# Gating weights read eight hidden blocks at a time in runs of 1 KB, two scale rows parked in memory, activations packed to 352 columns

## The reference, cut to what matters

```python
def peer(xn, w_pq, sub_keys, u, v):
    q = (xf @ w_pq).reshape(t, PEER_HEADS, 2, PEER_HALF)
    sc = jnp.einsum("thpd,hpnd->thpn", q, sub_keys).astype(jnp.float32)
    vals, idx = lax.top_k(sc, PEER_TOPK)
    ...
    best, pos = lax.top_k(cand, PEER_TOPK)
    eidx = jnp.take_along_axis(cidx, pos, axis=-1)
    g = jax.nn.softmax(best, axis=-1).astype(xn.dtype)
    ...
        ue = jnp.take(u, it, axis=0)
        act = jax.nn.gelu(jnp.einsum("td,tkd->tk", xt, ue), approximate=False) * gt
        ve = jnp.take(v, it, axis=0)
        return jnp.einsum("tk,tkd->td", act, ve)
...
        h = h + gate2 * peer(n2, w_pq[l], sub_keys[l], peer_u[l], peer_v[l])
    return rms_norm(h, g_final)
```

## Time and profile before

| | us |
|---|---|
| median of 3 runs | 1630.06 |
| lowest, highest | 1626.07, 1630.55 |
| profiled execution | 1628.63 |
| its span | 1626.8 |
| TensorE busy in it | 1587.6 |
| VectorE busy in it | 1382.7 |
| ScalarE, GpSimd busy in it | 643.2, 565.3 |
| mean granted TensorE clock | 0.987 |

### The profile page before, as it was taken

One profiled execution on the slowest core, in us unless ns is written; L12 is line 12 of the kernel. 1 busy time (PEld: TensorE's weight loads), 2 busy tenths in 40 slices (PEclk: granted clock), 3 DMA queues, 4 the chain that ended last, 5 costly groups with the idle time before them and its releaser, 6 DMA issues.

```text
span 1626.8 us, 23629 instructions
## 1 busy us (share of the span) xinstructions
PE 1587.6 (98%) x7941; PEld 1313.7 (81%) x7941; DVE 1382.7 (85%) x2751; ACT 643.2 (40%) x950; POOL 565.3 (35%) x479
## 2 busy tenths in 40 slices
PE   6999999999999999999999999999999999999997
PEld 4887764675556899988889888898988898888886
DVE  6788867765999999978989898989988888988886
ACT  3334654241112666663333333333333333333333
POOL 0000000011555300015555455554545566656510
PEclk7999999989999999999999999999999999999999
DMA  9522215532212255589999999999999999999981
GB/s 370 188 106 78 78 53 204 221 144 70 90 67 85 99 207 190 206 286 367 375 370 359 368 365 369 364 369 363 358 344 353 344 350 361 344 348 346 362 292 61
DMA packets 144460, 417.89 MB, mean 257 GB/s; under 512 B 11520, under 2 KB 56576, under 8 KB 138624
## 3 DMA queue, kind: packets, MB, share of 16 engines
q1 hardware_dynamic: 96128, 247.01, 42.2%
q0 software_dynamic: 47104, 167.83, 27.2%
q10 hardware_dynamic: 1152, 2.10, 0.3%
HBM read 389.59 MB, written 27.26 MB: 256 GB/s over the span
## 4 chain that ended last, share of the span: by engine, by line
PE 81%; DVE 12%; DMA 3%; issue 2%; ACT 1%; SPq 0%; DVEq 0%; ACTq 0%
PE ps L924 30%; PE ps L854 26%; PE ps L636 10%; PE ps L627 6%; PE ps L912 3%; PE ps L781 3%; DMA big<-pv 1%; DVE low L1768 1%; DVE att L1636 1%; DMA big<-wada 1%; DVE att L1647 1%; DVE big L1634 1%; DVE big L1652 1%; DVE low L1613 1%; DVE low L1761 1%
## 5 line engine op out<-in xcount | busy, mean ns | idle before, releaser
L924 PE MATMUL ps<-Vs,As 128*128 128x512 f32 x2286 | 538.6, 391 | 2.5 <-DVE As L1800 2.5
L924 PEld LDWEIGHTS ps<-Vs,As 128*128 128x128 f32 x2286 | 427.5, 188 | 87.7 <-DVE As L1800 2.8
L854 PE MATMUL ps<-xs,Us 128*128 128x352 f32 x2832 | 472.6, 322 | 2.3 <-DVE Us L1780 1.7
L854 PEld LDWEIGHTS ps<-xs,Us 128*128 128x128 f32 x2832 | 453.9, 188 | 16.1 <-DVE Us L1755 3.9
L565 POOL DMA_INDIRECT big<-pv,islot x160 | 235.0, 1468 | 163.4 <-DVE low L1839 77.7
L1279 ACT ACTIVATE att<-ps 128x384 f32<-128x384 f32 x96 | 47.2, 492 | 398.5 <-PE ps L854 398.4
L1797 DVE TENSOR_TENSOR Vs<-big,Vs 128x1024 fp32r<-128x1024 f32 x127 | 155.2, 1222 | 37.3 <-ACT Vs L1285 37.3
L627 PE MATMUL ps<-big 128*128 128x512 f32 (+1 forms) x416 | 161.1, 546 | 0.0
L1839 DVE SCALAR_TENSOR_TENSOR low<-big,act_w,low 128x1024 f32<-128x1024 f32 x128 | 157.3, 1279 | 0.0
L1285 ACT ACTIVATE Vs<-big 128x1024 fp32r<-128x1024 f32 x127 | 134.1, 1056 | 57.4 <-PE ps L924 40.8
L627 PEld LDWEIGHTS ps<-big 128*128 128x128 f32 x416 | 78.7, 192 | 74.0 <-issue 57.1
(11 more groups left out here) (234 smaller groups left out, 2044.4 us busy)
## 6 DMA issues: line engine op xcount, KB each, us to landing
big<-puT SPq DMA_DIRECT2D x128, 512.0 KB, 5.9
big<-pv SPq DMA_DIRECT2D x64, 1024.0 KB, 11.4
big<-stream SPq DMA_DIRECT2D x31, 1024.0 KB, 4.9
gmat<-big SPq DMA_DIRECT2D x11, 2048.0 KB, 7.3
att<-gmat SPq DMA_DIRECT2D x31, 704.0 KB, 13.9
low<-wada SPq DMA_DIRECT2D x28, 512.0 KB, 5.0
work<-wada SPq DMA_DIRECT2D x12, 512.0 KB, 4.9
big<-wada SPq DMA_DIRECT2D x8, 512.0 KB, 13.4
```

Source lines behind the costliest of these rows:

```text
L854: mm = nc.tensor.matmul(ps[:, 6 + e, XTOK:DT], a, xs[:, b, k, XTOK:DT], start=(k == 0 and a is hi and b == 0), stop=(k == KT - 1 and a is lo))
L924: mm = nc.tensor.matmul(ps[:, 2 * b + half, :], a, v_parts[:, w, half * T:(half + 1) * T], start=(opens and a is hi and w == 0), stop=(las ...
```

## The change

- A slot of `graw` holds eight blocks, not four: runs of 8 x 32 floats, 1 KB. It has no piece for the sparse tokens any more (FILLED = 11 instead of 12). A turn has two reads instead of four: for its blocks 8 to 15 at e == 0 (at e == 2 in the first turn), and for the next turn's blocks 0 to 7 at e == 5 (not in the last).
- `graw` grows to 5632 floats per partition and lies over `att`, `stats` and half of `rowv`. So `g2row` is stored to a fifth block of `hsave` by two transfers on ACT's queue right after it is made, and both `g2row` and `gfin` are read again in the last turn at e == 6, when slot 1 isn't needed any more. VectorE adds up `acc` at block 125 and does `residual(0)` at block 126. The first gating read waits for those stores and for the small copies of the indices (`ext_here`).
- The activations `early`, `gel`, `aside` and PSUM's hidden products are packed to 352 columns (ET); `gel` moves to `big`. The 32 columns of `As` and of `xs` that the output product reads for the sparse tokens are set to zero once, by ScalarE, and the `clear` matmuls go.

```diff
 XT = NK
+ET = DT - XTOK
...
 LATE = BODY - BODY // EVERY
+FILLED = PIECES - FIRST
+GRUN = 8
...
         colv = sb("colv", [P, 208])
-        rowv = sb("rowv", [P, HEADS + D])
...
         coef = sb("coef", [P, 2, KT])
-        stats = sb("stats", [P, 2 * T])
-        std, rstd = stats[:, 0:T], stats[:, T:2 * T]
...
         ptsb = sb("ptsb", [P, 2, 4, P])
+        place = ExitStack()
+        graw = place.enter_context(nc.sbuf_tensor("graw", [P, 2, FILLED, GRUN, HT], f32))
+        place.close()
         att = sb("att", [P, 8 * T])
+        stats = sb("stats", [P, 2 * T])
+        std, rstd = stats[:, 0:T], stats[:, T:2 * T]
+        rowv = sb("rowv", [P, HEADS + D])
...
         g2row = stats[:, :]
-        early = big[:, 10 * D:10 * D + EARLY * DT].rearrange("p (n t) -> p n t", n=EARLY)
+        early = big[:, 10 * D:10 * D + EARLY * ET].rearrange("p (n t) -> p n t", n=EARLY)
...
         ugap = [big[:, q * D:(q + 1) * D] for q in GPLACE]
-        aside = att[:, 1216:1216 + (GAP - KEPT) * DT].rearrange("p (n t) -> p n t", n=GAP - KEPT)
+        aside = att[:, 1216:1216 + (GAP - KEPT) * ET].rearrange("p (n t) -> p n t", n=GAP - KEPT)
...
         v_row = [row[:, q, :] for q in range(4)] + [big[:, (10 + q) * D:(11 + q) * D] for q in range(4)]
-        graw = att[:, 0:8 * DT].rearrange("p (s h a t) -> p s h a t", s=2, h=PIECES, a=4)
-        gel = att[:, 8 * DT:10 * DT].rearrange("p (s t) -> p s t", s=2)
+        gel = big[:, 21 * D:21 * D + 2 * ET].rearrange("p (s t) -> p s t", s=2)
...
         gel_ready, a_ready, ahi_ready, alo_ready = (sem(f"{w}_ready") for w in ("gel", "a", "ahi", "alo"))
-        idx_ready = sem("idx_ready")
+        idx_ready, g2_saved = sem("idx_ready"), sem("g2_saved")
...
                     sp.wait_ge(early_moved, 1)
-                    sp.dma_start(graw[:, 1, FIRST:PIECES - 2, :, :].rearrange("p h a t -> p h (a t)"),
-                                 gmat[FIRST:PIECES - 2, :, 0:4 * HT].rearrange("h p f -> p h f")).then_inc(g_here[1], 16)
+                    sp.wait_ge(ext_here, 16 * 2 * PH * NEXT)
+                    sp.wait_ge(g2_saved, 32)
+                    sp.dma_start(graw[:, 1, 0:FILLED - 2, :, :].rearrange("p h a t -> p h (a t)"),
+                                 gmat[FIRST:PIECES - 2, :, 0:GRUN * HT].rearrange("h p f -> p h f")).then_inc(g_here[1], 16)
...
             def load_g(g, q):
-                sp.wait_ge(a_ready, g * BODY + 4 * q + 4)
-                sp.dma_start(graw[:, (q + 1) % 2, FIRST:PIECES, :, :].rearrange("p h a t -> p h (a t)"),
-                             gmat[FIRST:PIECES, :, bass.ds((g * BODY + 4 * q) * HT, 4 * HT)].rearrange("h p f -> p h f")
+                sp.wait_ge(a_ready, g * BODY + q * GRUN)
+                sp.dma_start(graw[:, (q + 1) % 2, :, :, :].rearrange("p h a t -> p h (a t)"),
+                             gmat[FIRST:PIECES, :, bass.ds((g * BODY + q * GRUN) * HT, GRUN * HT)].rearrange("h p f -> p h f")
...
                 for e in range(BODY // 2):
+                    if last and e == 6:
+                        sp.wait_ge(a_ready, XT)
+                        sp.dma_start(g2row, hsave[:, TB * D:(TB + 1) * D]).then_inc(h_here, 16)
+                        sp.dma_start(gfin, rows[:, HEADS:HEADS + D]).then_inc(h_here, 16)
...
                             sp.wait_ge(piece_out[k], stored(PIECES + k))
-                    if e % 2 == 0 and not (first and e == 0):
-                        load_g(g, e // 2)
+                    if e == (2 if first else 0):
+                        load_g(g, 1)
+                    if e == 5 and not last:
+                        load_g(g, 2)
...
                 pool.wait_ge(xhi_ready, k + 1)
-                nc.gpsimd.tensor_tensor(xs[:, 1, k, :], nT[:, k, P:T], xs[:, 0, k, :].bitcast(f32), ALU.subtract
+                nc.gpsimd.tensor_tensor(xs[:, 1, k, XTOK:DT], nT[:, k, P + XTOK:T], xs[:, 0, k, XTOK:DT].bitcast(f32), ALU.subtract
...
                     for a, b in ((hi, 0), (hi, 1), (lo, 0)):
-                        mm = nc.tensor.matmul(ps[:, 6 + e, XTOK:DT], a, xs[:, b, k, XTOK:DT],
+                        mm = nc.tensor.matmul(ps[:, 6 + e, 0:ET], a, xs[:, b, k, XTOK:DT],
...
                 pe.wait_ge(gel_ready, n + 1)
-                mm = product(ps[:, gap_bank[n], XTOK:DT], lambda k: ugap[n][:, k * P:(k + 1) * P],
+                mm = product(ps[:, gap_bank[n], 0:ET], lambda k: ugap[n][:, k * P:(k + 1) * P],
...
-            def clear(e):
-
-                nc.tensor.matmul(ps[:, e, 0:XTOK], zeros[:, :], ones[:, 0:XTOK], start=True, stop=True)
-
-            clear(0)
-            clear(1)
...
                     pe.wait_ge(side_free, 2 * TB + 4)
-                    clear(6)
-                    clear(7)
...
                 act.wait_ge(n_ready, k + 1)
-                f(xs[:, 0, k, :], nT[:, k, P:T], ACT.Copy).then_inc(xhi_ready, 1)
+                f(xs[:, 0, k, XTOK:DT], nT[:, k, P + XTOK:T], ACT.Copy).then_inc(xhi_ready, 1)
+            f(xs[:, 0, 0:2, 0:XTOK], zeros[:, 0:2 * XTOK].rearrange("p (w t) -> p w t", w=2), ACT.Copy)
...
                 f(g2row[:, half * T:(half + 1) * T], ps[:, 6 + half, :], ACT.Copy).then_inc(side_free, 1)
+                act.wait_ge(side_free, half + 1)
+                act.dma_start(hsave[:, TB * D + half * T:TB * D + (half + 1) * T], g2row[:, half * T:(half + 1) * T]
+                              ).then_inc(g2_saved, 16)
...
                 act.wait_ge(u_done, n + 1 + 2)
-                f(aside[:, n - KEPT, :] if KEPT <= n < GAP else early[:, n, :], ps[:, gap_bank[n], 0:DT], ACT.Gelu
+                f(aside[:, n - KEPT, :] if KEPT <= n < GAP else early[:, n, :], ps[:, gap_bank[n], 0:ET], ACT.Gelu
...
                     act.wait_ge(g_taken, j + 1 + 4)
-                    f(graw[:, 1, PIECES - 2, :, :], piece[:, (PIECES - 2) % PRING, 0:4, :], ACT.Copy).then_inc(g_last, 1)
+                    f(graw[:, 1, FILLED - 2, :, :], piece[:, (PIECES - 2) % PRING, 0:GRUN, :], ACT.Copy).then_inc(g_last, 1)
...
             act.wait_ge(g_taken, BUILT + 4)
-            f(graw[:, :, 0:FIRST, :, :].rearrange("p s h a t -> p s (h a t)"),
-              zeros[:, :].unsqueeze(1).broadcast_to([P, 2, P]), ACT.Copy)
-            f(graw[:, 1, PIECES - 1, :, :], piece[:, (PIECES - 1) % PRING, 0:4, :], ACT.Copy).then_inc(g_last, 1)
+            for e in range(2):
+                f(As[:, e, :, 0:XTOK], zeros[:, 0:2 * XTOK].rearrange("p (w t) -> p w t", w=2), ACT.Copy)
+            f(graw[:, 1, FILLED - 1, :, :], piece[:, (PIECES - 1) % PRING, 0:GRUN, :], ACT.Copy).then_inc(g_last, 1)
...
                         act.wait_ge(alo_ready, o + (1 + 3 - before))
-                        f(gel[:, i % 2, :], ps[:, 6 + i % 2, 0:DT], ACT.Gelu).then_inc(gel_ready, 1)
+                        f(gel[:, i % 2, :], ps[:, 6 + i % 2, 0:ET], ACT.Gelu).then_inc(gel_ready, 1)
...
                     act.wait_ge(a_ready, o + (1 + 8))
-                    f(Al[:, 0, :] if last and d == BODY - 1 else As[:, d % 2, 0, :], act_t, ACT.Copy).then_inc(ahi_ready, 1)
+                    f(Al[:, 0, XTOK:DT] if last and d == BODY - 1 else As[:, d % 2, 0, XTOK:DT], act_t, ACT.Copy).then_inc(ahi_ready, 1)
...
                     act_t = gel[:, i % 2, :]
-                dve.wait_ge(g_here[(d // 4 + 1) % 2], g * 32 + (d // 8 + 1) * 16)
-                ga = act_t.rearrange("p (h t) -> p h t", h=PIECES)
-                v.tensor_tensor(ga, ga, graw[:, (d // 4 + 1) % 2, :, d % 4, :], ALU.mult).then_inc(a_ready, 1)
+                dve.wait_ge(g_here[(d // GRUN + 1) % 2], g * 16 + 16)
+                ga = act_t.rearrange("p (h t) -> p h t", h=FILLED)
+                v.tensor_tensor(ga, ga, graw[:, (d // GRUN + 1) % 2, :, d % GRUN, :], ALU.mult).then_inc(a_ready, 1)
...
                 dve.wait_ge(ahi_ready, o + 1)
-                v.tensor_tensor(A[:, 1, :], act_t, A[:, 0, :].bitcast(f32), ALU.subtract).then_inc(alo_ready, 1)
+                v.tensor_tensor(A[:, 1, XTOK:DT], act_t, A[:, 0, XTOK:DT].bitcast(f32), ALU.subtract).then_inc(alo_ready, 1)
...
                             add_row(r)
-                    if o == XT - 5:
+                    if o == XT - 3:
...
                         step(v.tensor_tensor(acc[:, 0, :], acc[:, 0, :], acc[:, 1, :], ALU.add))
-                        dve.wait_ge(h_here, 16 * TB)
-                    if o == XT - 4:
+                        dve.wait_ge(h_here, 16 * (TB + 2))
+                    if o == XT - 2:
...
     gmat = nc.dram_tensor("gmat", (PIECES, P, NK * HT), _mybir.dt.float32, kind="Internal").ap()
-    hsave = nc.dram_tensor("hsave", (P, TB * D), _mybir.dt.float32, kind="Internal").ap()
+    hsave = nc.dram_tensor("hsave", (P, (TB + 1) * D), _mybir.dt.float32, kind="Internal").ap()
```

## The result

The changed kernel takes 1743.84 us (median of 6 runs, 1741.09 to 1749.4), the kernel before 1629.88 (6 runs, 1626.07 to 1630.55): 1.0706 times as long, 95% interval 1.0688 to 1.0724. The forecast was 1633.5, its range ended at 1640. The change costs 114 us where the sum said 3.5.

A forecast was written before the change was run, and what follows sets the result against it. TensorE was taken to bound the dense stage, with transfers just keeping up. Stall +1.7, steady -0.9, tail +2.4 and its clock +0.3 summed to +3.5 us on the 1630.06 median: 1633.5 us, range 1626 to 1640.

The forecast's parts named there:

- What bounds the kernel: Dense stage: TensorE sets the pace, transfers just keep up; faster transfers can give back only 2.7 us in the steady part.
- The gating reads: Steady part: half the runs save 1.0 us of transfer time a turn; -0.9 us taken, bounds -2.7 and +1.
- the price of a 1 KB run: Gating reads: estimated 44 ns per 1 KB run against 25 ns per 512-byte run, between 40 and 50.
- The place where it hurts: Start, pv rows of blocks 4 and 5: doubled read lengthens TensorE's stall from 2.5 to 4.2 us; +1.7, bounds 0 and 3.4.
- The clock's 1.9 us: Start: loss from TensorE's lowered clock behind the 2.5 us stall, 18 output products in 5.98 us; kept unchanged.
- The tail: Last blocks: `residual(0)` at block 126 delays ScalarE's Square and the end, +2.4 us; TensorE's clock falling behind it, +0.3.
- the slower rival: Reads at e == 0 and e == 5: half of 14 loads behind them stall 1 us; +10.5, 1640.5 us, chance 0.16.
- the bound of +1 us: Steady part: upper bound of the gating-read term, in case a doubled read makes one block late.
- The faster rival: Half the runs lose half the turns to gathered rows; start's 5.4 and steady 2.7 us vanish: -5.7, 1624.4 us, chance 0.15.
- The change doesn't do what it says: Gating reads: a 1 KB run costs two of 512 bytes, 50 ns; steady 0, start +2.2: +4.9, 1635.0 us, chance 0.09.

The follow-up runs named there:

- the kernel with both moved: The changed kernel with the e == 0 read moved to e == 2 and the e == 5 read to e == 6: 1637.34 us, ratio 1.0047.
- the one with the first read moved as well: Changed kernel, reads at e == 2 and e == 6, the first turn's read behind the `peer_v` load of e == 3: 1631.69 us, ratio 1.0008.

## Why the prediction was wrong, by its own steps

**What bounds the kernel.** Right, and it was the trap. From TensorE at 836.31 of 837 us I took that transfers had slack, and asked only how far longer transfers would use it up. The row says that in the old order nothing is late. It doesn't say how much each load can be delayed in a new order, and a full TensorE has no way to take a stall back.

**The gating reads: -0.9 us.** Not contradicted, once the two misplaced reads were moved, and no more than that: from the pair at 770.22 to the last in the pattern at 1610.0 the kernel with both moved takes 839.8 us, against 840.7 before. But the same stretch is 840.3 us in the kernel that differs from the one before only in its tail, and 841.1 us in the one with the first read moved as well. Nor is the price of a 1 KB run borne out: in the first read alone, 1 KB runs moved 276 GB/s on average (703 to 705 us of the kernel after, with 0.91 of the engines' time), which doesn't exceed the plateau of the 512-byte ones.

**The place where it hurts: +1.7 us.** The place was right, the size wasn't: from the beginning of the stall up to the first undisturbed pair the kernel with both moved takes 3.9 us more than the one before. The stall is 5.52 us instead of 2.5; `peer_v` landed 25.12 us after its issue instead of 22.06. These two traces flatter the term. Over the four that share this start with the kernel after, the landing is 26.1 us in the mean, and over the three that share it with the kernel before 21.4: +4.8 us where I took 1.7 and set 3.4 as the upper bound. Why the added bytes cost that much no run shows. The clock's 1.9 us grew to 2.8 (18 products in 6.89 us).

**The tail: +2.4 and +0.3 us.** Right: 26.0 us from the last hidden product's end to the end of the span, where 23.1 were, +2.9; done alone in the kernel before it costs about 2. The path was right only where the clock stays up, as in the kernel after (25.4 us, +2.3, the chain through ScalarE's Square). Where it falls (18 products in 6.00 us in the kernel with both moved) the chain goes through TensorE's slow products instead.

**The sum of these** is 3.9 - 0.9 + 2.9 = 5.9 us, and the kernel with both reads moved is 1636.0 - 1626.8 = 9.2 longer in its profiled execution. The other 3 us lie ahead of the dense stage, where the profiled executions of kernels built on the one after begin about 2 us later on average. 2.6 of them are there before the first instruction that the change adds: the products of L618 start at 347.93 us before and at 350.56 (L631) in the kernel with both moved. Over all traces they start at 347.9 to 349.3 us in kernels built on the one before and at 348.6 to 351.5 in the others. I did not find a cause; it is no larger than the spread between executions.

**The step that failed: the slower rival, at 0.16 and 10.5 us.** It named the mechanism in its first half, "the doubled reads delay a pv block in each turn beyond its slack", and even the place, "the loads behind the reads at e == 0 and e == 5, 14 of them". All 14 stalled. In the sum these stalls had no term but the bound of +1 us, "a doubled read makes one block late". The rival failed in three points of its working:

- It counted only what a read adds to the landing behind it, and not the wait in front of the read. The change part lists `g * BODY + q * GRUN` beside `g * BODY + 4 * q + 4`; worked out at q = 1, g = 1 the one is block 15 and the other, at q = 0, block 11, and the load behind it needs block 13. SP's queue is in order: 15 us of standing. That is the 61.6 us, of which 25 are the wait's alone.
- It took the slack from one row, 4.4 us at 1505.09, for all loads. That is an even pair's. Reads had so far stood only ahead of even pairs; e == 5 is an odd one, with 15 us and not 22 from issue to stall. That, with twice the bytes in the read, is the 42.1 us.
- It priced a stall at 1 us, for half of them. They idled 5.1 us on average and then lost about 2 us more each to the clock (13 of the 14), which the earlier trace rows had already shown behind 2.5 us of idleness.

**The faster rival**, that half the runs are half the turns lost to gathered rows: there may be something in it, as two reads of 512-byte runs took 5.5 us more than one of 1 KB runs with the same bytes; but that run also has twice the transfers. And the change puts twice the bytes at the start, and the steady part had nothing to gain. **The change doesn't do what it says**, a 1 KB run at the price of two of 512 bytes: open, for the same reason; by its own working it moves the sum by 1.4 us only.

## What to carry to other kernels

When loads share an in-order queue, write out for every load which block its wait is for, before and after the change, and for the load behind it: a wait that is later than its successor's holds the successor, and nothing in the old profile warns of it. A load that is moved takes its delay to a new successor, so measure that one's slack (issue to landing, landing to the first stall) and not the slack of the one it stood ahead of. And a TensorE that is busy throughout shows that the present order is good, not that there is room: price a stall with its idle time and with the low clock that can follow it.

## What the runs showed that I had not expected

At the start no order of the same loads removed the lost time: with the doubled read ahead of `peer_v` TensorE idled 5.5 to 7.3 us, with it behind (and so ahead of puT) 4.5 and 5.7, each time for whichever came last. Only a read taken out of that stretch removed it.

A load of 1 MB right behind a read of 1408 KB took 13 to 21 us to land in the steady part of the kernel after, and 25 to 27 at the start of the kernels built on it, where the engines are full (1.01 of their time at 404 GB/s from 750 to 762.4 us of the kernel after, 1.03 in the kernel before).

Every stall of 3.65 us or more ahead of output products was followed by a low granted clock: 18 of them in 6.96 us behind 4.51 us of idleness, in 5.92 behind 6.96, against 4.11 in the steady part. Between 1.9 and 3.5 us it went either way: 5.97 us behind 1.94, 5.83 behind 2.26 and 7.09 behind 3.38, but the clock stayed full behind 2.19, 2.39, 3.39 and 3.50. Where it fell the price was 1.6 to 3.2 us, and it doesn't grow with the stall.
